# A rebuilt trunk scan in a hybrid decoder step: decay weights from per-head rows, five steps instead of six, norm moved to the next group

## What is computed

```python
def ssd_chunk(h, x, dt, A, bm, cm):
    cum = jnp.cumsum(dt * A, axis=1)
    seg = cum[:, :, None] - cum[:, None, :]
    decay = jnp.exp(jnp.where(causal, seg, -jnp.inf))
    cb = jnp.einsum('btgn,bsgn->btsg', cm, bm)
    w = cb[..., None] * decay * dt[:, None]
    y = jnp.einsum('btsgh,bsghp->btghp', w, x)
    y = y + jnp.einsum('btgn,bghpn->btghp', cm, h) * jnp.exp(cum)[..., None]
    tail = jnp.exp(cum[:, -1:] - cum) * dt
    h_new = jnp.exp(cum[:, -1])[..., None, None] * h + jnp.einsum('bsgh,bsgn,bsghp->bghpn', tail, bm, x)
    return h_new, y
...
a = glu_v * jax.nn.sigmoid(glu_g)
a = causal_dwconv(a_full, conf_dw_w, conf_dw_b)                 # 31 taps
xbc = jax.nn.silu(causal_dwconv(xbc_full, ssm_conv_w, ssm_conv_b))   # 4 taps
y, h = ssd(xs_h, dt, A, bm, cm, h0g, lead)
y = y + d_skip * xs_h
y = y * jax.nn.silu(z)
yg = yg * lax.rsqrt(jnp.mean(yg * yg, axis=-1, keepdims=True) + EPS)  # per group of 256 channels
y = yg * ssm_norm_w
```

## Time and profile before

| | |
|---|---|
| median of 3 runs | 1776.57 us (1765.78 to 1777.68) |
| span of the profiled execution | 1770.0 us; no time of its own is listed beside it |
| between that span and the median | 6.6 us |
| mean granted clock | 0.903 of full speed |
| trunk loop, 8 groups | 82.3 to 982.8 us |

### The profile page before, as it was taken

How to read it: one execution, slowest core, us unless ns; L and a number is a source line. 1 busy time by engine, 2 the same in 40 slices (tenths; PEclk the granted TensorE clock), 3 DMA queues, 4 the chain that set the end, 5 groups by cost and what they waited for, 6 DMA issues and landing times. The chain is left out here.

```text
span 1770.0 us, 27567 instructions
## 1 busy us (share of the span) xinstructions
PE 1465.9 (83%) x8979; PEld 1283.1 (72%) x8979; DVE 1348.9 (76%) x2060; ACT 727.2 (41%) x1012; POOL 395.0 (22%) x467
## 2 busy tenths in 40 slices
PE   3898988989889899898998499998338888888880
PEld 2896887968879688796887389986336777676760
DVE  4169888888888888888888636442738999999984
ACT  3132232322323223232232322332028888888871
POOL 1035243352433424334252000000130000000002
PEclk9599897998989989899799699999669999999995
DMA  4031241411414115141160644320359999999966
GB/s 135 24 96 32 79 107 49 130 44 50 135 47 121 54 45 140 40 128 54 42 179 13 202 143 151 120 78 12 105 210 370 369 372 370 370 371 373 369 241 226
DMA packets 187558, 274.00 MB, mean 155 GB/s; under 512 B 11196, under 2 KB 149670, under 8 KB 172118
## 3 DMA queue, kind: packets, MB, share of 16 engines
q1 hardware_dynamic: 174638, 231.85, 40.0%
q10 hardware_dynamic: 8672, 27.86, 4.0%
q0 software_dynamic: 4208, 13.78, 2.2%
HBM read 224.19 MB, written 50.12 MB: 155 GB/s over the span
## 5 line engine op out<-in xcount | busy, mean ns | idle before, releaser
L731 PE MATMUL pu<-xh,wh 128*128 128x304 f32 (+1 forms) x1280 | 289.2, 309 | 5.8 <-ACT zc L651 4.6
L731 PE MATMUL pu<-xl,wh 128*128 128x304 f32 (+1 forms) x1280 | 279.8, 301 | 0.0
L731 PE MATMUL pu<-xh,wl 128*128 128x304 f32 (+1 forms) x1280 | 278.1, 300 | 0.0
L731 PEld LDWEIGHTS pu<-xh,wh 128*128 128x128 f32 x1280 | 206.9, 199 | 10.2 <-issue 9.9
L731 PEld LDWEIGHTS pu<-xl,wh 128*128 128x128 f32 x1280 | 208.7, 199 | 0.0
L731 PEld LDWEIGHTS pu<-xh,wl 128*128 128x128 f32 x1280 | 206.0, 198 | 0.0
L1965 DVE TENSOR_TENSOR W13l<-W,W13h 128x1024 fp32r<-128x1024 f32 x160 | 185.2, 1221 | 11.3 <-ACT W13h L1913 10.7
L230 POOL TENSOR_TENSOR wl<-ring,wh 128x1024 fp32r<-128x1024 f32 x48 | 118.8, 2475 | 330.2 <-ACT wh L504 330.2
L871 DVE SCALAR_TENSOR_TENSOR cacc<-a_p,gc,cacc 128x528 f32<-128x528 f32 x232 | 187.4, 808 | 0.0
L504 ACT ACTIVATE wh<-ring 128x1024 fp32r<-128x1024 f32 x80 | 84.5, 1057 | 218.4 <-PE pu L731 218.3
L1872 PE MATMUL eh<-W13h,xch 128*128 128x512 f32 x320 | 130.6, 408 | 50.5 <-DVE xcl L1965 46.2
(11 more groups left out here) (381 smaller groups left out, 3195.9 us busy)
## 6 DMA issues: line engine op xcount, KB each, us to landing
W<-in_exp_w SPq DMA_DIRECT2D x120, 1024.0 KB, 8.2
ring<-in_w_in SPq DMA_DIRECT2D x80, 512.0 KB, 3.9
slot_rows<-yo ACTq DMA_DIRECT2D x40, 512.0 KB, 8.6
x<-in_state_ssm SPq DMA_DIRECT2D x16, 512.0 KB, 7.0
out_new_ssm_sample<-x SPq DMA_DIRECT2D x16, 512.0 KB, 5.3
wraw<-in_ssm_out_w SPq DMA_DIRECT2D x8, 1024.0 KB, 8.2
gates<-gbuf ACTq DMA_DIRECT2D x16, 280.0 KB, 2.1
ssd_rows<-yout SPq DMA_DIRECT2D x8, 560.0 KB, 2.9
```

The costliest lines, as they stand in the source:

```text
L731: last = pe.matmul(u_cols(r, a, b), w[:, k % RING, j, :], x[:, j, a:b], start=(j == 0 and n == 0), stop=(j == KD - 1 and n == 2))
```

## The change

All of it is in the trunk.

- **Steps.** The 16 meta columns and the 32 sample columns become one step of 48 (`S0`), masked by block; five steps (`STEPS`) instead of six, samples first.
- **Decay weights.** The prologue computes, in rows per head (32 partitions x 560 columns), the cumulative decay and `v = ln(dt) - cum`, each in a high and a low half, and stores them in DRAM (`seg`). SP's `rows_in` loads a group's rows into `rows`. PE forms `cum[t] + v[s]` with products of four rows (one for each head) on top of a product that adds a mask of -1e30 above the diagonal; the exponential then is decay times dt, ready. The decay columns come from `rows` too, by products of two rows. POOL's `aUh`, `aUl`, `ab`, `xtl`, DVE's `cbm`, `xdt` go; `xtl` (with the last column of `Lx`) and `hTd` move from POOL to DVE; `Lx` times C·B reads `pT` in PSUM and writes `Wx`.
- **Convolutions.** The first of the 4 taps, with its bias, is now an ACT operation on PSUM with a scale and a bias for each channel; the skip term `d_skip * x` is an ACT operation (`skip`); one of 31 taps of the branch is too. The branch's sample columns are done by one product over a sliding view (8 sequences x 4 rows x 31 taps) and one reduction. 14 of the taps (`EARLY`) and the end (`conf_done`) move to the next group's front.
- **Norm.** The sums over y, the root (`sums_out`), the reciprocal and the scaling (`normalise`) move to the next group's front: on PE behind block 1, on ACT between `silu(0)` and `silu(1)`, on DVE before the third convolution. A copy `gcc` of the group's constants outlives `gc`.
- **Order.** `U_OF` becomes `[0, 1, 4, 5, 8, 9, 10, 11, 12, 13]`: blocks 0, 1, norm sums, blocks 2, 3, decay columns, blocks 4 to 9. Block 4 stands before `stage1(0)`, blocks 5 to 9 go between the scan's parts.
- **POOL's order.** The split of block 4 follows a wait on `s_cconv` (the previous group's branch done, now in this group) and two copies; the split of block 5 follows `Bblk`, which waits for step 0's transposes.
- **States.** ACT scales the samples' states by their decay (`h0_decay`, 16 operations of 128 x 128); DVE adds with four operations of 128 x 512.

The core of the diff:

```diff
-CHUNKS = [(0, SAMP), (SAMP, META)] + [(SAMP + META + CHUNK * i, CHUNK) for i in range(SEQ // CHUNK)]
-ORDER = [1, 2, 3, 4, 5, 0]
+S0 = SAMP + META
+STEPS = [(0, S0)] + [(S0 + CHUNK * i, CHUNK) for i in range(SEQ // CHUNK)]
+EARLY = [[0, 1, 2, 3, 4], [5, 6, 7, 8], [9, 10, 11, 12, 13]]
+LATE = list(range(14, CK - 2))
-U_OF = [0, 1, 2, 3, 4, 5, 8, 9, 10, 11]
+U_OF = [0, 1, 4, 5, 8, 9, 10, 11, 12, 13]
...
 # SP, group
-                blocks(g, range(RING, 6))
+                blocks(g, range(RING, 4))
+                if isinstance(g, int) and g == 0:
+                    rows_out()
+                rows_in(g)
+                blocks(g, range(4, 6))
                 if not isinstance(g, int) or g > 0:
                     results_out(g - 1)
+                conf_out(g)
...
 # POOL, group
+                pool.tensor_copy(gc[:, :], cs[:, g, :]).then_inc(s_gc, 1)
+                split(g, 2)
+                split(g, 3)
+                pool.wait_ge(s_cconv, g + 1 + 1)
+                pool.tensor_copy(gcc[:, :], cs[:, g, :]).then_inc(s_gcc, 1)
+                pool.tensor_copy(a_s[:, :, 0:CK - 1], ...).then_inc(s_stc, 1)
                 split(g, 4)
+                pool.wait_ge(s_T, STEP * g + 1 + 1)
+                pool.tensor_tensor(Bblk, Bs..., Bm..., ALU.mult).then_inc(s_Bblk, 1)
                 split(g, 5)
...
 # ACT, group
+                    evac(r)
                     split_behind(q)
                     act.activation(raw_p[:, q, SK - 1:], u_cols(r, SAMP, T), ACT.Copy).then_inc(s_raw, 1)
+                    act.activation(cv[:, q, :], u_cols(r, 0, T), ACT.Identity, scale=gc[...], bias=gc[...]).then_inc(s_ufree, 1)
...
                 raw(0)
                 raw(1)
+                silu(0)
+                sums_out()
+                silu(1)
                 raw(2)
+                skip(0)
+                silu(2)
                 raw(3)
+                skip(1)
+                for i in range(2):
+                    decays(i)
+                silu(3)
+                evac(8)
                 split_behind(4)
                 act.activation(zc[:, 0, :], u_cols(0, 0, T), ACT.Copy, scale=0.5).then_inc(s_ufree, 1)
                 chunk(0)
+                evac(9)
+                split_behind(5)
+                act.activation(zc[:, 1, :], u_cols(1, 0, T), ACT.Tanh, scale=0.5).then_inc(s_ufree, 1)
+                chunk(1)
...
 # PE, group
+                block(0)
+                block(1)
+                pe.wait_ge(s_sq2, g + 1)
+                sums(U0, g)
+                block(2)
+                block(3)
+                pe.wait_ge(s_rows, 64 * g + 64)
+                for i in range(2):
+                    decay_cols(i)
+                block(4)
                 stage1(0)
+                block(5, (0,))
                 stage2(0)
                 stage1(1)
+                block(5, (1,))
                 stage2(1)
                 stage1(2)
...
 # PE, the log decay of a step
+                    pe.matmul(v, identR[0:S, 0:S], (neg0R if j == 0 else negR)..., start=True, stop=False)
+                    for h in range(HG):
+                        last = pe.matmul(v[:, h, :], rows[q:q + 4, 1, h, a:a + S], rows[q:q + 4, 0, h, a:a + S],
+                                         start=False, stop=(h == HG - 1))
...
 # DVE, group
+                early(0)
                 dve.wait_ge(s_gc, g + 1)
+                ssm_conv(0)
+                conf_samples()
+                silu(0)
+                early(1)
+                ssm_conv(1)
+                silu(1)
+                early(2)
+                normalise(g)
+                ssm_conv(2)
+                conf_done(g)
+                silu(2)
+                ssm_conv(3)
                 silu(3)
+                stage1(0)
                 split(6)
+                stage2(0)
+                stage1(1)
```

More of the change, by code:

```diff
@@ L282, in states_in, with rows_out, rows_in @@
                     sp.dma_start(h0[:, i], src[g, i]).then_inc(s_h0, 16)
+            def rows_out():
+                sp.wait_ge(s_hi, 2)
+                sp.wait_ge(s_lo, 2)
+                for kind, pair in enumerate(((cum_h, cum_l), (v_h, v_l))):
+                    for x in range(2):
+                        sp.dma_start(keep["seg"][kind, x], pair[x].bitcast(F32)).then_inc(s_rst, 16)
+                sp.wait_ge(s_rst, 64)
+                sp.sem_inc(s_yz, 1)
+            def rows_in(g):
+                sp.wait_ge(s_cstr, 1)
+                sp.wait_ge(s_pe1, STEP * g + 1)
+                for q, (c, W) in enumerate(QCOLS):
+                    for kind in range(2):
+                        src = keep["seg"][kind][:, bass.ds(HG * g, HG), c:c + W]
+                        p0 = 32 * q + 2 * kind
+                        sp.dma_start(rows[p0:p0 + 2, kind, :, 0:W].bitcast(F32), src).then_inc(s_rows, 16)
             def results_out(g):
@@ L560, in silu, with skip, sums_out @@
                     act.activation(th[:, q % 2, :], cv[:, q, :], ACT.Tanh).then_inc(s_thx, 1)
+                def skip(q):
+                    act.wait_ge(s_cv, 4 * g + q + 1)
+                    act.wait_ge(s_yz, g + 1)
+                    act.activation(ybuf[:, q, :], cv[:, q, :], ACT.Copy, scale=gc[:, R_DS + q:R_DS + q + 1]).then_inc(s_dx, 1)
+                def sums_out():
+                    for r in range(2):
+                        evac(2 + r)
+                        act.activation(rs[:, 280 * r:280 * r + 280], pu[r][:, 0:280], ACT.Sqrt,
+                                       scale=1.0 / (2 * P), bias=eps[:, :]).then_inc(s_ufree, 1)
@@ L856, in _ @@
                 pe.transpose(pY[0:62, 2 * P:3 * P], pa[:, :], ident[:, :]).then_inc(s_out, 1)
-                pe.wait_ge(s_sq2, g + 1)
-                for r in range(2):
-                    free(12 + r)
-                    for i in range(2):
-                        last = pe.matmul(pu[r][:, 0:280], ones[:, :], th[:, i, 280 * r:280 * r + 280],
-                                         start=(i == 0), stop=(i == 1))
-                    last.then_inc(s_u, 1)
+            pe.wait_ge(s_tot, 1)
+            pe.wait_ge(s_fillfree, 17)
+            pe.matmul(pT[:, 0:4 * NH], ones[0:NH, :], tot[:, :, :].rearrange("k c h -> k (c h)"),
+                      start=True, stop=True).then_inc(s_tp, 1)
+            pe.wait_ge(s_te, 1)
+            pe.wait_ge(s_cstr, 5)
+            with pe.Fori(0, G) as g:
+                group(g)
+            pe.wait_ge(s_sq2, G + 1)
+            pe.wait_ge(s_ufree, U_TILES * G + 2)
+            sums(0, None)
         @block.vector
@@ L1059, in _ @@
                 stt(a_p[:, CK - 1:], zc[:, 1, SAMP:T], 1.0, zc[:, 0, SAMP:T], ALU.add, ALU.mult).then_inc(s_ga, 1)
-                dve.wait_ge(s_ga, 2 * g + 2)
                 split(7)
-                tap = iter(range(CK))
+                stage2(1)
+                stage1(2)
+                dve.wait_ge(s_c0, g + 1)
+                late = LATE + (sum(EARLY, []) if is_last else [])
+                tap = iter(late)
                 def taps(n):
                     for _ in range(n):
-                        conf_tap(next(tap))
@@ L1068, in _ @@
-                taps(2)
-                stage1(0)
-                taps(2)
-                stage2(0)
-                for j in range(1, 6):
-                    stage1(j)
-                    if j in (1, 3):
-                        split(8 + j // 2)
-                    if j < 5:
-                        taps(2)
-                        stage2(j)
+                        conf_taps([next(tap)])
+                taps(1)
+                stage2(2)
+                stage1(3)
+                taps(1)
@@ L1113 @@
+            with dve.Fori(0, G - 1) as g:
+                k.enter(g, DVE_STEPS)
+                group(g)
+                k.leave(G - 1)
+            group(G - 1, is_last=True)
+            normalise(G, last=True)
+            conf_samples()
+            conf_done(G)
+OT = [(0, SAMP)] + STEPS[1:]
 NT = len(OT)
```

704 lines of the change are left out of this document (351 added, 353 removed).

## The result

The change makes the kernel slower: a median of 1855.45 us (1851.94 to 1857.76, 4 runs) against 1771.71 us for the kernel before (1765.78 to 1777.68, 4 runs); the ratio is 1.0484, with a 95% interval of 1.045 to 1.0518. The forecast was 1830 in a range of 1735 to 1872, slower. The profiled execution has a span of 1855.5 us, against 1770.0 before: 85.5 us to account for.

A forecast was written before the change was run, and what follows sets the result against it. PE, issuing in order, sets the period: 89.0 us work, 23.9 idle, 5.2 and 2.0 clock give 120.1 a group. Loop +57, prologue -10, epilogue +8 make +55 on 1776.6: 1830 us, range 1735 to 1872.

The forecast's parts named there:

- the walk: One trunk group followed from block 0's start through the engines' instruction orders: 89.0 us PE work plus 23.9 idle.
- rival (c): Trunk, worse: clock also lost after third pause, sliding view costs twice, or block 6's load late; 1850 to 1862; chance 0.14.
- The front: From block 0 to block 4: ACT's and POOL's paths both give block 4 at 41.7 us; PE idles 14.0.
- `silu(1)` needs the tanh table again, 1.28 us, and ends at 24.7: ACT in the front: reloading the tanh table after the norm's square root was counted on the path.
- The tie of ACT's and POOL's paths: Before block 4: ACT's `decays(0)` ends at 41.7 us and POOL's split of block 4 at 41.6.
- Blocks 4 and 5: Block 5 starts 6.7 us after block 4, behind POOL's `Bblk` and split; PE idles 6.0 us.
- Step 1's pause: Before stage 2 of step 1: ACT does `evac(9)` before `chunk(1)`, so PE waits 3.9 us.
- Four-row products: PE's weights of a step: one product of 512 columns and four of 128, taken as 0.95 us.
- rival (d): PE's steps of four rows take as long as full ones: +2.2 us a group; no separate chance given.
- The clock after the third pause: Behind the pause before stage 2 of step 1: no clock loss charged; 5.2 us charged after the first two.
- Rival (a): Trunk: waits as walked but the clock costs nothing extra; 1778 to 1795 us; chance 0.17.
- Rival (b): Trunk: DVE's front is off the path and PE bounds the loop; 1650 us, half of it 1725; chance 0.20 with halves.

The follow-up runs named there:

- e3_split4: Against the changed kernel, POOL splits block 4's weights right behind block 3's, ahead of its wait for the conformer convolution; 1862.37 us.
- e1_split5: Against the changed kernel, POOL splits block 5's weights right behind block 4's, ahead of its wait for the first transposed chunk and `Bblk`; 1828.79 us.
- e2_chunk1: Against the changed kernel, ACT does the chunk of step 1 before evacuation 9 in place of after; 1794.08 us.
- e6_front: Against the changed kernel, DVE's front reordered (convolutions 1 and 2 earlier, norm and remaining early taps later) and block 4's weights split early on POOL; 1829.02 us.
- e7_all: e6_front plus block 5's weights split behind block 4's on POOL and ACT's chunk of step 1 ahead of evacuation 9; 1764.27 us.
- e5_warm: Against the changed kernel, dummy products added in PE's three pauses of a group (66, 44 and 26), nothing else; 1813.69 us.
- e4_norecip: Against the changed kernel, the reciprocal in the gated norm (3.65 us of DVE a group) left out, so the norm is not computed; 1823.43 us.
- e8_tail: The changed kernel with the edits of e1_split5 and e2_chunk1 together, front as in the change; 1771.35 us.
- e9_load6: e7_all with SP's loads of blocks 6 and 7 ahead of the stores of the norm's and the conformer's results; 1711.32 us.
- e12_raw3: e9_load6 with ACT's front reordered: block 3's copies ahead of convolution 2's tanh, block 5's weight copy and skip term behind the decays; 1708.39 us.

## Why the prediction was right, and where it was off

The way and the place of the loss came out as forecast: three pauses of PE, in the places named and by the instruction orders named. (The first was to be 10 us or more, released by ACT's `Ed` or POOL's `wl`; it is 12.1 us in four parts, and the large one, 8.96, stands before the second decay product and is released by `raw(3)`, as the walk has it.) The size did not quite: 1855 lies above the forecast's own band (1795 to 1850), in that of rival (c) (1850 to 1862), which had a chance of 0.14. By kind, a group has 89.8 us of PE's own work (walked 89.0), 21.4 of idle time (23.9) and 11.6 lost to the clock (7.2).

**The front** (block 4 at 41.7): measured 40.7. With block 0 at 560.10: third convolution's end 36.4 (walked 37.5), `conf_done` 37.3 (38.6), `raw(3)` 39.4 (40.5), POOL's split 40.6 (41.6). Up to the end of the second convolution (22.9, walked 22.7) the walk is within 0.2 us; from `silu(1)` on it puts everything 1.0 too late. The step that failed there is "`silu(1)` needs the tanh table again, 1.28 us, and ends at 24.7": ACT loads the table at 577.75, ahead of its wait for the convolution, and still waits 3.99 us after it. The load was off the path. The samples, taken at 2.4 between 1.3 and 4.9, measured 1.18 + 1.19. The tie of ACT's and POOL's paths held: e3_split4 gained nothing. Idle before block 4 is 12.1, not 14.0: block 4 starts 1.0 earlier, and PE's own work ahead of it takes 28.6 us in place of 27.7.

**Blocks 4 and 5**: block 4 8.9 us (8.8), block 5 15.86 behind block 4's start (15.5), by the queue order named, which e1_split5 confirms. Step 1's pause 3.60 (3.9), by the order named; e2_chunk1 confirms it. **Four-row products**: mask and four products take 1.01 us (622.50 to 623.51), taken as 0.95; rival (d) falls.

**The clock after the third pause.** "None after the third, since pauses of up to 2.3 us left the clock at 1.00" is the step that failed. It cost 4.3 (e2_chunk1) to 4.9 us (windows) a group. The rows that it rested on showed pauses of up to 2.3 us in busy stretches; here one of 3.6 us ended a stretch of 21.3 us in which PE worked 12.0. And they were not all the rows: the trace of before has the clock falling right behind a pause of 1.88 us, where the tail with its 0.70 begins:

```profile
724.73 0.66 PE L771 MATMUL pY<-Lx,xdt 128*64 128x128 f32 x8 [1.88 <-DVE Lx L1016]
```

```profile
720.73:724.73 4.00, 2.12 (x17) 1.89 (x15) 3.67 (x10) 1.83 (x3) 2.36 (x4) 1.00 0.39 114
724.73:728.73 4.00, 3.60 (x21) 2.00 (x21) 3.50 (x9) 0.35 (x2) 0.20 (x1) 0.63 0.18 72
```

The other terms of the clock held: 3.3 and 1.8 us behind the first two pauses (2.6 each), 1.7 in the tail (2.0). From block 5 to the group's end it makes 66.3 us where 62.9 were walked. Together: 120.1 - 1.0 + 0.4 + 3.4 = 122.9, the measured 122.85. That is rival (c) in its first part, which the prediction priced at 2.6 us and gave too little weight (the late load of block 6, another part of it, did not come in the change, but did, at 5.0 and 5.5 us, in e6_front and e7_all); the Trainium skill's sentence named in the prediction pointed to it. Rival (a), no price for the clock, is refuted by e2_chunk1 and e5_warm. Rival (b), DVE's front off the path, is refuted by e4_norecip.

**The sums.** From the first block to the last added state the loop grew by 975.5 - 891.1 = 84.4 us, against +57 predicted: 10.3 x 8 = 82 from the period, the rest at the ends of the cut. Of the 27 us between, 22 are the period (122.85, walked 120.1), and 4 are a slip of the prediction, which called 120.1 - 112.5 = 7.6 us "7.1". The prologue is 13.2 us shorter (block 0 at 69.1, before 82.3; predicted -10, in bounds). The epilogue from the last added state to the trunk's last store (1070.61) grew from 17.8 to 26.0, +8.2 (predicted +8). From that store to the end it takes 784.9 us where it took 778.8, +6.1, in code that the change does not touch. The variants fall on either value (e2_chunk1 778.8, e8_tail 779.4, e1_split5 785.2, e9_load6 784.5), so it does not belong to the change; its cause was not looked for. Sum: 84.4 - 13.2 + 8.2 + 6.1 = 85.5, where the prediction had 55: 30.5 us more. The median is only 25 us above the forecast because that was counted from a median 6.6 us above the span, and rounded down by 1.6. Those 5 us are luck. Luck too is that two misses of the walk stood against each other, the table load (8 us too many) and the stretch with the third pause (27 too few).

## What to carry to other kernels

Work taken off DVE, POOL and PE bought nothing in this order of instructions, because each engine's hand-written order put a short wait in front of something that another engine needed; in order of price here: a chunk behind an evacuation on ACT (7.4 us a group), loads behind stores on SP (6.7, once the front is early), the norm ahead of a convolution on DVE (3.4), a split behind a product on POOL (3.0). When the front of an in-order pipeline is pulled earlier, walk the DMA queue too: its waits were hidden only by the lateness of the rest. And price a pause of PE with the half-clock stretch behind it; here taking 3.1 us off one pause gave 7.4 (e2_chunk1).

## What the runs showed of the hardware that was not expected

- A pause of 3.60 us, at the end of 21.3 us in which PE was busy for 12.0, was followed by 9.8 us at 1.2 GHz with PE busy throughout. After the first pause (8.96) the clock was back 5.7 us after block 4 began.
- The length of a pause alone does not tell what follows. Before stage 2 of step 0, 1.41 us in e1_split5 were followed by 6.8 us at 0.50, and 1.44 us in e9_load6 left the clock at 1.00; in the kernel before, 2.26 us left it at 1.00 and 1.88 us did not. In e12_raw3, with pauses of 1.03, 0.62 and 2.21, windows of 4 us in the front still show 0.70 and 0.66. No run here isolates what decides.
- The clock also falls where the profile shows PE busy without a pause: in the change it is at 0.50 from about 668 to 671.4, 0.9 us behind the 32 products of 4 columns (663.60, 3.63 us).
- ACT's table load can stand ahead of the wait of the instruction that needs it (577.75, with 3.99 us of waiting behind it), and then it is free. It does not always: in the kernel before, the load at 651.46 came behind a wait of 6.64 us for PE, with the split behind it. Read from the trace on which side of the wait it is.
- Taps on DVE with a scalar operand and two tile operands lose 2.0 us to a split of 2.9 us on POOL; DVE and POOL share even where neither is busy on average (65% and 12%).
